# A two-block transformer kernel on one core: loads, stores and small preparations moved at seven part boundaries

## The reference

```
for i in 0, 1:                       # first block
    mod   = silu(c) @ ada_w[i] + ada_b[i]        # shift, scale, gate; the same for c_ctx
    h, hc = x*(1+scale)+shift, ctx*(1+scale_c)+shift_c
    p, z  = split(h @ w_in)                      # w_in: attention (i=0), S5 (i=1)
    y     = attention(p, pc)  or  s5(p, pc)      # S5: diagonal state-space model, then gelu
    x     = layer_norm(alpha*x + gate*((y*silu(z)) @ w_out[i]))   # ctx too for i=0
# S5 ends with y = g * sigmoid(g @ glu_w + glu_b)
for layer in 0, 1:                   # second block
    x += even_mixer(rms_norm(x))  or  gla_mixer(rms_norm(x))
    x += conv_ffn(rms_norm(x))
```

## Time and profile before

| | us |
|---|---|
| median of 3 runs | 1612.75 (1611.44 to 1613.54) |
| the profiled execution | 1618.0 |
| its span in the profile | 1616.2 |
| busy in the span: TensorE | 1537.4 (95%) |
| VectorE | 981.2 (61%) |
| ScalarE | 790.6 (49%) |
| GpSimd | 648.1 (40%) |

### The profile page before, as it was taken

How to read it: one execution, slowest core, us unless ns; L and a number is a source line. 1 busy time by engine, 2 the same in 40 slices (tenths; PEclk the granted TensorE clock), 3 DMA queues, 4 the chain that set the end, 5 groups by cost and what they waited for, 6 DMA issues and landing times. The chain is left out here.

```text
span 1616.2 us, 28573 instructions
## 1 busy us (share of the span) xinstructions
PE 1537.4 (95%) x11512; PEld 1320.7 (82%) x11512; DVE 981.2 (61%) x1368; ACT 790.6 (49%) x1072; POOL 648.1 (40%) x497
## 2 busy tenths in 40 slices
PE   5999999899899899999989999989999999999998
PEld 2777788588787688888889977879999877789997
DVE  6577422689644349668656557736666665466675
ACT  4412222566412578787554345735554364454542
POOL 0589799599399792578311116010000100210000
PEclk9999999999999899999999999989999999999999
DMA  9889978665434578988885446224545242355440
GB/s 381 311 301 299 343 250 260 214 208 179 153 140 169 172 251 233 275 244 266 210 301 195 179 163 216 106 104 187 231 156 208 94 157 104 131 210 207 183 172 36
DMA packets 120593, 331.33 MB, mean 205 GB/s; under 512 B 33800, under 2 KB 73480, under 8 KB 104224
## 3 DMA queue, kind: packets, MB, share of 16 engines
q1 hardware_dynamic: 116740, 287.69, 52.0%
q10 hardware_dynamic: 3740, 42.05, 7.0%
HBM read 283.49 MB, written 37.83 MB: 199 GB/s over the span
## 5 line engine op out<-in xcount | busy, mean ns | idle before, releaser
L3532 PE MATMUL ffn_ps<-ffn_x_lead,w_lead 128*128 128x256 f32 x672 | 188.4, 280 | 1.1 <-DVE w_rest L3611 1.1
L3532 PE MATMUL ffn_ps<-ffn_x_lead,w_rest 128*128 128x256 f32 x672 | 188.6, 281 | 0.0
L3532 PE MATMUL ffn_ps<-ffn_x_rest,w_lead 128*128 128x256 f32 x672 | 188.3, 280 | 0.0
L414 POOL TENSOR_TENSOR w_rest<-resident_ring,w_lead 128x2048 fp32r<-128x2048 f32 x7 | 32.1, 4592 | 387.8 <-ACT w_lead L410 200.1
L3611 DVE TENSOR_TENSOR w_rest<-resident_ring,w_lead 128x2048 fp32r<-128x2048 f32 x42 | 96.1, 2292 | 83.8 <-ACT w_lead L3576 83.8
L3532 PEld LDWEIGHTS ffn_ps<-ffn_x_lead,w_lead 128*128 128x128 f32 x672 | 126.1, 188 | 2.1 <-issue 1.4
L3532 PEld LDWEIGHTS ffn_ps<-ffn_x_rest,w_lead 128*128 128x128 f32 x672 | 126.4, 188 | 0.7
L3532 PEld LDWEIGHTS ffn_ps<-ffn_x_lead,w_rest 128*128 128x128 f32 x672 | 126.3, 188 | 0.0
L284 DVE TENSOR_TENSOR w_rest<-resident_ring,w_lead 128x2048 fp32r<-128x2048 f32 x33 | 78.1, 2370 | 63.9 <-ACT w_lead L278 63.5
L3576 ACT ACTIVATE w_lead<-resident_ring 128x2048 fp32r<-128x2048 f32 x42 | 80.1, 1912 | 50.7 <-PE ffn_ps L3532 50.6
L284 DVE TENSOR_TENSOR qkvz_w_rest<-resident_ring,qkvz_w_lead 128x2048 fp32r<-128x2048 f32 x20 | 53.6, 2679 | 83.2 <-ACT qkvz_w_lead L278 83.2
(11 more groups left out here) (619 smaller groups left out, 4646.8 us busy)
## 6 DMA issues: line engine op xcount, KB each, us to landing
resident_ring<-in_ffn_gu SPq DMA_DIRECT2D x22, 2048.0 KB, 9.0
ffn_wd<-in_ffn_down SPq DMA_DIRECT2D x22, 1024.0 KB, 4.8
xc<-s_q_scratch SPq DMA_DIRECT2D x128, 128.0 KB, 3.5
resident_ring<-in_ada_w ACTq DMA_DIRECT2D x8, 2048.0 KB, 8.7
resident_x<-in_s_bT SPq DMA_DIRECT2D x64, 256.0 KB, 4.3
resident_ring<-in_attn_w_in ACTq DMA_DIRECT2D x8, 2048.0 KB, 9.0
s_W_scratch<-resident_x SPq DMA_DIRECT2D x64, 256.0 KB, 4.4
resident_ring<-in_s_w SPq DMA_DIRECT2D x32, 512.0 KB, 6.4
```

What stands on the lines that cost most here:

```text
L414: self.core.nc.gpsimd.tensor_tensor(self.slots[1][0], self._raw(r), self.slots[0][0].bitcast(F32), ALU.subtract).then_inc(self.rest_made, 1)
L3532: last = nc.tensor.matmul(ps[s][f][:, m, :], w_part[w][m][:, k, f * P:(f + 1) * P], x_part[x][:, k, :], start=(k, w, x) == (0, 0, 0), stop ...
```

## The change

- Opening: x and ctx are loaded by SyncE behind the four ada_w tiles instead of by ScalarE. The tables' groups 0 and 1 follow tile 1, groups 2 and 3 tile 2, the others tile 3, on TensorE and ScalarE alike, and the semaphore `powers` counts finer. The last `pick_sums` stands behind the last tables.
- `W_QKVZ`: 39 becomes 38.
- V: the buffers that are stored lie first in `residual_normalized`, where the ring V begins in `s5_mixer`; the semaphores are the core's. The wait for their stores moves from the end of the part to `s5_mixer`, on SyncE in turn 1 and on GpSimd at tile 2, the first that writes there (the ring's order is reversed).
- The third quarter of g is split in `s5_gate`; one `spin(8)` becomes `spin(6)`; weight unit 2 is split before the loop.
- `even_mixer`: GpSimd waits for all of `weighed` before `early.rest`. Both mixers: `spin(3)` between the first transposes and the products. `odd_mixer`: the gate weights are split after the first four input parts.

```diff
@@ start_scalar, start_vector(..., then=None)
             if norm is not None and piece < 2:
                 norm.leads(act, piece)
+            if piece == 0 and then is not None:
+                then()
@@ tables
-ADA_TABS = {2: (0, 1, 2, 3), 3: (4, 5, 6)}
-ADA_EMPTIED = {2: (0, 1), 3: (2, 3, 4, 5, 6)}
+ADA_TABS = {1: (0, 1), 2: (2, 3), 3: (4, 5, 6)}
@@ modulation, SyncE (the same three loads leave ScalarE)
+                for t in range(LT):
+                    sp.dma_start(core.x[:, t, :], d["x"][t * P:(t + 1) * P, :]).then_inc(s_const, 16)
+                sp.dma_start(xc[:], d["ctx"].rearrange("(t p) n -> p t n", p=P)).then_inc(s_const, 16)
                 for s in range(2):
                     sp.wait_ge(mm_done, NT - 2 + s)
                     core.load(sp, s, d["attn_w_in"][s])
@@ modulation, TensorE
-                    if g == NT - 1:
-                        pick_sums(g)
                     for n in ADA_TABS.get(g, ()):
                         tab_tensor(pe, n)
+                pick_sums(NT - 1)
@@ tables, TensorE and VectorE
-        if n == 0:
-            pe.wait_ge(powers, 1)
-        if n == 4:
-            pe.wait_ge(powers, 2)
+        if n in (0, 1, 2, 4):
+            pe.wait_ge(powers, {0: 1, 1: 2, 2: 3, 4: 4}[n])
...
         for n in (1, 2, 4):
             product([(pw[:, n:2 * n], slice(0, P))], pw[:, n - 1, 0, :], pw[:, n - 1, 1, :], pw[:, 0:n], n)
-        dve.sem_inc(powers, 1)
+            dve.sem_inc(powers, 1)
@@
-W_QKVZ = 39
+W_QKVZ = 38
@@ residual_normalized, SyncE
-                quads.last(sp)
@@ EarlyQuads
+    @classmethod
+    def stored(cls, core, eng):
         for s in range(2):
             for c in range(2):
-                sp.wait_ge(self.out[s][c], 16 * (self.count // 2))
+                eng.wait_ge(core.V_stored[s][c], 16 * len(cls.TILES))
@@ s5_mixer, SyncE in later_loads(1); then GpSimd; then TensorE, ScalarE, VectorE at the end
                             c_load(k)
+                        EarlyQuads.stored(core, sp)
...
+                    if k == 2:
+                        EarlyQuads.stored(core, pool)
...
-                return V[:, 2 * SLOT[k] + h]
+                return V[:, 2 * (2 - SLOT[k]) + h]
...
                 turn_outputs(CT)
-                spin(nc, ps_u, core.ident, 8)
+                spin(nc, ps_u, core.ident, 6)
...
-                gate_input_lead(2)
...
-                gate_input_rest(2)
@@ s5_gate (ScalarE; VectorE alike with rest)
-        late = slice(3 * HT, ET)
+        late = [slice(i * HT, (i + 1) * HT) for i in (2, 3)]
...
-                        if u == 0 and k == 3 * HT:
-                            pe.wait_ge(g_rest_made, 1)
+                        if u == 0 and k in (2 * HT, 3 * HT):
+                            pe.wait_ge(g_rest_made, k // HT - 1)
...
-                nc.scalar.activation(parts[0][:, late], gT[:, late], ACT.Copy).then_inc(g_lead_made, 1)
-                lead(1)
+                for ks in late:
+                    nc.scalar.activation(parts[0][:, ks], gT[:, ks], ACT.Copy).then_inc(g_lead_made, 1)
+                for u in (1, 2):
+                    lead(u)
...
-                    if 0 < u < ET - 1:
+                    if 1 < u < ET - 1:
                         lead(u + 1)
@@ even_mixer, GpSimd
+                pool.wait_ge(weighed, 2 * HP)
                 early.rest(pool, 0)
@@ even_mixer and odd_mixer, TensorE
                 norm.transposes(pe, 0)
+                spin(nc, ps[0][0], core.ident, 3)
@@ odd_mixer, ScalarE (VectorE alike with gate_weights_rest)
-                act.wait_ge(xl, 16)
-                sc.activation(xw_parts[0][:], xw[:], ACT.Copy).then_inc(xw_lead, 1)
-                split.start_scalar(act, norm)
+                def gate_weights_lead():
+                    act.wait_ge(xl, 16)
+                    sc.activation(xw_parts[0][:], xw[:], ACT.Copy).then_inc(xw_lead, 1)
+                split.start_scalar(act, norm, gate_weights_lead)
```

More of the change, by code:

```diff
@@ L85, in __init__ @@
         self.tables_stored = ctx.enter_context(nc.semaphore("tables_stored"))
+        self.V_stored = [many(f"V_stored{s}", 2) for s in range(2)]
         self.spent = []
@@ L288, in _x_pieces, with start_scalar @@
         return range(2 * self.halves) if self.src is not None else ()
-    def start_scalar(self, act, norm=None):
+    def start_scalar(self, act, norm=None, then=None):
         for piece in range(2 * self.halves):
@@ L304, in start_scalar, with start_vector @@
                 self.core.nc.scalar.activation(self.lhs[0][:, to], self.src[:, ks], ACT.Copy).then_inc(self.x_lead_made, 1)
-    def start_vector(self, dve, norm=None):
+    def start_vector(self, dve, norm=None, then=None):
         for piece in range(2 * self.halves):
@@ L629, in _ @@
                 tab_scalar(act)
-                for t in range(LT):
-                    act.dma_start(core.x[:, t, :], d["x"][t * P:(t + 1) * P, :]).then_inc(s_const, 16)
-                act.dma_start(xc[:], d["ctx"].rearrange("(t p) n -> p t n", p=P)).then_inc(s_const, 16)
                 def keep(g):
@@ L638, in _ @@
                     keep(g)
-                    for n in ADA_EMPTIED.get(g, ()):
+                    for n in ADA_TABS.get(g, ()):
                         tab_empty(act, n)
@@ L1243, in residual_normalized @@
     with phase(core, name) as ph:
+        quads = EarlyQuads(core, ph)
         gate = ph.sb("gate", [P, 2, DM])
@@ L1255, in residual_normalized @@
                       first=[first[:, :, 2 + i, :] for i in range(2)])
-        quads = EarlyQuads(core, ph)
         more = [(ln_g[:], d["ln_gT"]), (ln_b[:], d["ln_bT"]), *again]
@@ L1701, in __init__ @@
         self.core = core
+        core.V_at = core.nc.sbuf_base
+        self.v = [[ph.sb(f"vp_v{s}{c}", [P, 4 * P]) for c in range(2)] for s in range(2)]
         self.ptab = ph.sb("vp_ptab", [P, 3, CH, 2, QG])
         self.cc = ph.sb("vp_cc", [P, 2, 2, P])
-        self.v = [[ph.sb(f"vp_v{s}{c}", [P, 4 * P]) for c in range(2)] for s in range(2)]
         self.tmp = ph.sb("vp_tmp", [P, 4 * P])
@@ L1707, in __init__ @@
         self.c_in = [ph.sem(f"vp_c_in{s}") for s in range(2)]
-        self.out = [[ph.sem(f"vp_out{s}{c}") for c in range(2)] for s in range(2)]
+        self.out = core.V_stored
         self.count = 2 * len(self.TILES)
@@ L1724, in turn @@
             self.c_load(sp, n // 2 + 2)
-    def last(self, sp):
+    @classmethod
+    def stored(cls, core, eng):
         for s in range(2):
             for c in range(2):
-                sp.wait_ge(self.out[s][c], 16 * (self.count // 2))
+                eng.wait_ge(core.V_stored[s][c], 16 * len(cls.TILES))
     def make(self, pool):
@@ L1811, in s5_mixer @@
         g_parts = [m[:].rearrange("p k n -> p (k n)").rearrange("p (k n) -> p k n", k=ET) for m in hparts]
+        hs = ph.sb("hs", [P, 2, QG, LC])
+        assert nc.sbuf_base == core.V_at
+        V = ph.sb("V", [P, RING, 2, 4, P])
         us = [ph.sb(f"us{s}", [P, CH, NCH]) for s in range(2)]
@@ L1817, in s5_mixer @@
         apow_raw = ph.sb("apow", [P, 2, LEVELS, 3, QG])
-        hs = ph.sb("hs", [P, 2, QG, LC])
-        V = ph.sb("V", [P, RING, 2, 4, P])
         ptab, ptab_last = ph.sb("ptab", [P, 2, CH, 2, QG]), ph.sb("ptab_last", [P, CH, 2, QG])
@@ L2582, in y_rest @@
                     v.tensor_tensor(y_parts[1][:, u, :], yz[:, u % 2], y_parts[0][:, u, :].bitcast(F32), ALU.subtract).then_inc(y_rest_made, 1)
-                dve.wait_ge(g_lead_made, 1)
-                v.tensor_tensor(parts[1][:, late], gT[:, late], parts[0][:, late].bitcast(F32), ALU.subtract).then_inc(g_rest_made, 1)
-                rest(1)
+                for i, ks in enumerate(late):
+                    dve.wait_ge(g_lead_made, i + 1)
+                    v.tensor_tensor(parts[1][:, ks], gT[:, ks], parts[0][:, ks].bitcast(F32), ALU.subtract).then_inc(g_rest_made, 1)
+                for u in (1, 2):
+                    rest(u)
                 dve.wait_ge(z_in, 16)
                 for u in range(ET):
-                    if 0 < u < ET - 1:
+                    if 1 < u < ET - 1:
                         rest(u + 1)
@@ L3372, in gated, with gate_weights_rest @@
                     last.then_inc(out_done, 1)
-                dve.wait_ge(xw_lead, 1)
-                v.tensor_tensor(xw_parts[1][:], xw[:], xw_parts[0][:].bitcast(F32), ALU.subtract).then_inc(xw_rest, 1)
-                split.start_vector(dve, norm)
+                def gate_weights_rest():
+                    dve.wait_ge(xw_lead, 1)
+                    v.tensor_tensor(xw_parts[1][:], xw[:], xw_parts[0][:].bitcast(F32), ALU.subtract).then_inc(xw_rest, 1)
+                split.start_vector(dve, norm, gate_weights_rest)
                 dve.wait_ge(std, 1)
```

## The result

The changed kernel takes 1590.93 us (median of 4 runs, 1584.38 to 1591.13), the kernel before 1612.1 us beside it (4 runs, 1610.8 to 1613.54). The ratio is 0.984, with a 95% interval of 0.982 to 0.987. Measured again against 17 other runs of before it is 0.986 (0.983 to 0.988). Of 1612 us these ratios are 25 and 23 us; the medians themselves lie 21.2 and 24.0 us apart. Forecast were 25.1 us and 1587.7 us. The profiled execution has a span of 1589.3 us and a mean granted clock of 0.991.

A forecast was written before the change was run, and what follows sets the result against it. TensorE was taken as the bound, losing time where it stands still or works at 1.2 GHz. Seven places sum to 25.1 us, taking the plain median of 1612.75 to 1587.7 us; the forecast's own range is 1584 to 1591.5.

The forecast's parts named there:

- 1, opening: Kernel's start: x and ctx behind the tiles and spread tables start the next part at 35.2 instead of 39.45: 4.2 us.
- rival B: Opening doesn't move, as ScalarE's tables or the first projection tile end as late as now: 1591.9 us, chance 0.08.
- 2, projection's end: Projection to attention: one block less lets TensorE end last, 2.3 us, and the clock holds, 1.0 us.
- 3, V's stores: Output to state-space part: no wait for the last store, 3.8 us, and less half clock, 0.4 us.
- C: Slower: V's late stores hold the state-space part; 1627.7 us if they land 60 us after issue; chance 0.02.
- the 3.8: State-space part's start: without the wait for V's last store it starts at about 524.1 instead of 527.94, 3.8 us.
- 4, end of the state-space part and gate: Third quarter moved and fewer fillers, 0.8 us; third weight half ready before TensorE asks, gate net 1.2 us.
- 5, even mixer's start: Three fillers in the 1.47 us gap before the first product hold the clock: 1.2 us (0 to 1.7).
- 6, even mixer's end: GpSimd's wait for `weighed` removes a 2.7 us pause and the half clock after it: 7.5 us (2.7 to 7.8).
- D: Even mixer: GpSimd's late wait makes its subtraction the last; the place gives 5 or so, 1590 us; chance 0.05.
- A: Clock falls anyway at attention's start and in the mixers, losing 8.4 us of clock: 1596.1 us, chance 0.18.
- 7, odd mixer's start: Gate weights behind the first four parts start the product earlier, 1.3 us; 1.4 us more if the clock holds.

## Why the prediction was right, and where its steps were not

The total is right: 25.1 us forecast, 25 and 23 by the two ratios, 23.8 by the parts. Of the 3.2 us between 1587.7 and the median of 1590.9, 1.3 are the parts' sum; the rest is within the spread of both kernels (1612.75 was the base, and the medians of before were 1612.1 to 1616.6).

- **1, opening:** 4.2 forecast, 3.3. The first transpose moved by 4.1 as worked out. The step that failed is "the first projection tile comes next: 34.6": it landed at 36.28, and ScalarE's queue has the tile's split ahead of the values. That costs 0.8 to 0.9 us, a small part of what rival B feared (4.2).
- **2, projection's end:** 3.3 forecast, 2.8 (1.7 + 1.0, the clock mostly in the latter). The mechanism is shown by the dose of 40 blocks. The 2.3 was read off one profile; over the profiles with 39 blocks the gap is anything from 0.3 us, which is none, to 4.7.
- **3, V's stores:** 4.2 forecast, 3.2 (2.8 + 0.4). The late waits cost nothing, as said, and C has nothing for it. What was mis-sized is the 3.8: the next part started 4.5 us behind GpSimd's last operation in the profile that was read, but 3.0 to 4.5 over five, and without the wait TensorE ends the part in four of eight profiles.
- **4, end of the state-space part and gate:** 2.0 forecast, 2.3 (1.3 + 1.0). The gap of 1.73 us that the gate's term was read from is in two of the five profiles without the edit; the other three have 0.60.
- **5, even mixer's start:** 1.2 forecast, nothing. The step "if the clock holds, the first twelve products end 1.7 us sooner" took for the rule a fall that was there in one profile of seven.
- **6, even mixer's end:** 7.5 forecast, 8.1: pause 2.5, clock 5.6. GpSimd's late subtraction was hidden, so D didn't happen, and A is refuted where most of it lay.
- **7, odd mixer's start:** 2.7 forecast, 4.0. The start itself gave 2.9 (8.07 to 5.21 us); the rest is the later fall of the clock, which was in no step. The prediction credits the clock's 1.4 us to the fillers; they come with the weights' order alone as well.

Two errors of more than a microsecond, at 5 and 7, nearly cancel, and that the total lies so close is luck to that extent. The sum was safer than its terms.

## What to carry to other kernels

Look for the pause that stands ahead of work at half clock: here filling it with idle products brought 5.6 of 8.1 us, and moving GpSimd's subtraction, which held up the multiply, brought all 8.1. Before counting a fall of the clock as removable, see whether it is in a second profile, and whether TensorE is last in that part at all. And where single executions differ by more than the effect, compare parts between the same marks in several profiles. That told 0.1 us here in the stretches that repeat, and about 1 us in the others, while whole times couldn't tell the 2.3 us of the gate's edits from nothing.

## What the runs showed of the hardware that was not expected

TensorE stalls in a long unrolled stretch of small products for up to 4.4 us at a time with no releaser, and 47 of 48 stalls end 2.2 to 2.7 us after a 16 KB packet of the instruction queue starts. They stand only at places that are multiples of 126 to 127 matmuls apart, and these places move by as many matmuls as are added ahead of them. In a profile they add up to 1.9 to 11.0 us, and the three with the most (8.0, 9.3 and 11.0) have the longest middles of the part (265.9, 266.8 and 273.5 us). That the packets carry TensorE's code is inferred from this. The Trainium skill (Advanced Engine Details and Errata, ISA Cache) gives a cache line of 16 KB for 256 instructions; the packets' size agrees, and so does the distance, as 126 to 127 matmuls with their weight loads are 252 to 254 instructions.

The clock behaves differently in holding and in coming back: the even mixer's tail ran 9 us at 1.00 when it began so, and 13 us at 0.50 when it began with that, with the same work.
